# Rows of experts added up one pair behind their dots, ahead of each engine's step of the second half

## The chip, the cores and the metric

One core of a Trainium2 chip runs one program. TensorE (PE) multiplies, VectorE (DVE) does elementwise work, dot products and sorting, ScalarE (ACT) activation functions and scaled copies, GpSimd (POOL) issues the gathers, SyncE (SP) issues the weight loads. Each engine runs its own list of instructions in order and waits on semaphores for the others. The metric is the device time of the whole program in microseconds, the median of several executions.

## The reference

A block of layers over 512 tokens of width 1024: a short-convolution mixer and a feed-forward layer, a state-space mixer and a feed-forward layer, and then a hybrid layer of banded attention, a gated delta rule and a product-key layer of single-neuron experts. The change touches how the last two are interleaved. The product-key layer, cut to what matters (128 tokens in a block; 8 heads with 16 experts each):

```python
experts = jnp.take_along_axis(cand_i, pos, axis=-1)       # (128, 8, 16) of 16384
gates = jax.nn.softmax(top_s, axis=-1)
u  = expert_down[experts]                                 # a row of 1024 each
vv = expert_up[experts]
act = jax.nn.gelu(jnp.einsum("thkd,td->thk", u, hb))
out = jnp.einsum("thk,thkd->td", gates * act, vv)
```

So each of 4 blocks of 128 tokens has 128 experts per token. For each of them a row of 2048 numbers per token (`u` and `vv` side by side) is fetched, the first half is dotted with the token's vector, the result goes through GELU and the gate, and the second half is added to the output with that factor.

## The kernel before, in words

Everything is f32. After the first layers the hybrid layer is computed in two halves of 256 tokens. `pe_main(e, f)`, `act_main(e, f)` and `dve_main(e, f)` are generators: they give the work of half f on each engine in steps, and a step of one engine waits on semaphores for what the others made. Half 0 runs alone. Its tokens are blocks c = 0 and 1 of the experts; half 1 makes blocks 2 and 3. So while half 1 is still computed, the experts of block 0 and of part of block 1 are worked off between its steps.

`pe_experts`, `act_experts` and `dve_experts` write out that interleaving by hand. Block c has 64 rounds; a round `grp` handles a pair of experts per token (`GG = 2`), n = 128 c + 2 grp. In a round:

- POOL (`pool_gather`, a list of its own of 512 gathers) has fetched two tiles of 128 rows of 8 KB, 1 MB each, into a ring of buffers. Gather n waits until `g_mm` of the gather that had the buffer before it. Up to gather 255 there are `NRING = 7` buffers; from 256 on there are twelve, since five more have been freed by half 1.
- DVE: `dve_dots` (two CUSTOM instructions of 1024 elements, L187) waits for each gather and makes two columns of dots.
- ACT: `act_gelu` (128x2) waits for both dots. DVE: `dve_gate` (128x2 TENSOR_TENSOR, L170) multiplies by the gates. ACT: `act_diag` makes two 128x128 identities scaled by the factor of each token (L164, `arena<-arena,tail 128x128`).
- PE: `pe_add` (L153, `psum<-tail,arena ... 128x512`) multiplies each identity with the second half of its tile, two products of 512 columns each, and adds to two PSUM banks; f32 products count as two instructions in the profile, so the add of a pair is x8. Its end is `g_mm`, which frees the buffer.

Between them stands `steps_of(c, grp, main, ranks)`, a step of half 1 and steps of the ranking of the next block (`dve_topk`, 32 steps of top-16 searches on DVE; on PE and ACT it is nearly all waiting steps). In block 0 a round takes one step of half 1 (every fourth round two) and two of the ranking. In block 1 it takes half 1's steps first, and when they are at an end, the ranking for block 2; in block 2, the ranking for block 3. The ring of scaled identities has eight entries, that of dots eight pairs.

The order within a round is:

- PE: step, then `pe_add(grp)`.
- ACT: `act_gelu(grp)`, step, `act_diag(grp)`.
- DVE: `dve_dots(grp)`, step, `dve_gate(grp)`.

After the 64 rounds of a block, `pe_finish`, `act_finish` and `dve_finish` scale the sum, add the residual and free the PSUM banks; `store` is issued by ACT in round 4 of the next block (by SP for the last block). SP's list of weight loads (`sp_load`) knows nothing of rounds: it issues a load when the products that used the buffer are done.

Of the kernel before, what the change touches and what calls it, by code (L numbers as in the profile page):

```python
# [226 lines left out]
def build(nc, t, out):  # L227
    ctx = ExitStack()
    with ctx:
# [970 lines left out]
        def wait_steps(n):  # L1200
            for _ in range(n):
                yield
# [783 lines left out]
        def pe_tok(e, c):  # L1986
            for u in range(2):
                key = "htk", c, u
                o = ps.claim(key, QGB)
                e.wait_ge(*ps.vacant(key))  # L1990
                e.wait_ge(*t_h.at((5, c // 2, 7)))
                for k in range(4):
                    ins = e.tr(o[:, part[k]], H[:, 4 * u + k, part[c % 2]], ident)
                ins.then_inc(*tk_pe.tick((c, u)))
                yield
            yield

        def act_tok(e, c):
            yield
            for u in range(2):  # L2000
                e.wait_ge(*tk_pe.at((c, u)))
                if c > 1:
                    e.wait_ge(*g_dot.at(128 * (c - 2) + 127))
                e.act(htk[c % 2][:, 512 * u:512 * u + 512], ps["htk", c, u], ACT.Copy).then_inc(*ps.release(("htk", c, u)))
                yield
# [14 lines left out]
        def act_topk(e, c):  # L2020
            yield from wait_steps(31)
            e.wait_ge(*k_dve.at((c, "gate_in")))
            e.act(gates[c % 2], gates[c % 2], ACT.Exp).then_inc(*k_gate.tick(c))
            yield
# [125 lines left out]
        GROUPS = 128 // GG  # L2150
# [37 lines left out]
        def act_gelu(e, c, grp):  # L2188
            n = 128 * c + GG * grp
            d = dots[(n // GG) % 8]  # L2190
            e.wait_ge(*g_dot.at(n + GG - 1))
            e.act(d, d, ACT.Gelu).then_inc(*g_gelu.tick(n))

        def act_diag(e, c, grp):
            n = 128 * c + GG * grp
            d = dots[(n // GG) % 8]
            e.wait_ge(*g_act.at((c, grp)))
            for i in range(GG):
                if n + i >= 8:
                    e.wait_ge(*g_mm.at(n + i - 8))  # L2200
                e.act(diag[(n + i) % 8], ident, ACT.Copy, scale=d[:, i:i + 1]).then_inc(*g_diag.tick(n + i))

        def pe_add(e, c, grp):
            for i in range(GG):
                s_i = GG * grp + i
                n = 128 * c + s_i
                if s_i == 0:
                    for u in range(2):
                        ps.claim(("acc", c, u), (u,))
                        e.wait_ge(*ps.vacant(("acc", c, u)))  # L2210
                e.wait_ge(*g_in.at((c, s_i)))
                e.wait_ge(*g_diag.at(n))
                for u in range(2):
                    ins = e.mm(ps["acc", c, u], diag[n % 8], SLOTS[slot_no[n]][:, 1024 + 512 * u:1536 + 512 * u],
                               s_i == 0, s_i == 127)
                ins.then_inc(*g_mm.tick(n))

        def pe_finish(e, c):
            for u in range(2):
                o = ps.claim(("gB", c, u), HB)  # L2220
                e.wait_ge(*ps.vacant(("gB", c, u)))
                e.wait_ge(*der_ok.at((5, "post")))
                for k in range(4):
                    ins = e.mm(o[:, part[k]], post(5, 4 * u + k).broadcast_to([128, 128]), ident)
                ins.then_inc(*f_pe.tick(("gB", c, u)))
                o = ps.claim(("xo", c, u), HB)
                e.wait_ge(*ps.vacant(("xo", c, u)))
                for k in range(4):
                    ins = e.tr(o[:, part[k]], xT[:, 4 * u + k, 128 * c:128 * c + 128], ident)
                ins.then_inc(*f_pe.tick(("xo", c, u)))  # L2230

        def act_finish(e, c):
            for u in range(2):
                e.wait_ge(*f_pe.at(("gB", c, u)))
                if c:
                    e.wait_ge(*stored.at((c - 1, u)))
                e.act(fin_out[:, 512 * u:512 * u + 512], ps["gB", c, u], ACT.Copy).then_inc(*ps.release(("gB", c, u)))
# [13 lines left out]
        def store(e, c):  # L2251
            for u in range(2):
                e.wait_ge(*ps.done(("xo", c, u)))
                e.dma(out[0, 128 * c:128 * c + 128, 512 * u:512 * u + 512], fin_out[:, 512 * u:512 * u + 512]).then_inc(
                    *stored.tick((c, u), u))
# [10 lines left out]
        def steps_of(c, grp, main, ranks):  # L2266

            if c == 0:
                some(ranks, 2)
                some(main, 2 if grp % 4 == 3 else 1)  # L2270
            elif c == 1 and next(main, True) is None:
                pass
            else:
                some(ranks, 1)

        def pe_experts(e):
            main = pe_main(e, 1)
            before_rows(main, iter(()))
            for c in range(4):
                ranks = iter(()) if c == 3 else wait_steps(32)  # L2280
                late = pe_tok(e, 3) if c == 2 else iter(())
                for grp in range(GROUPS):
                    steps_of(c, grp, main, ranks)
                    next(late, None)
                    pe_add(e, c, grp)
                pe_finish(e, c)

        def act_experts(e):
            main = act_main(e, 1)
            before_rows(main, iter(()))  # L2290
            drive(act_topk(e, 0))
            for c in range(4):
                ranks = iter(()) if c == 3 else act_topk(e, c + 1)
                late = act_tok(e, 3) if c == 2 else iter(())
                for grp in range(GROUPS):
                    act_gelu(e, c, grp)
                    steps_of(c, grp, main, ranks)
                    next(late, None)
                    if c and grp == 4:
                        store(e, c - 1)  # L2300
                    act_diag(e, c, grp)
                act_finish(e, c)

        def dve_experts(e, ranks):
            main = dve_main(e, 1)
            before_rows(main, ranks)
            drive(ranks)
            for c in range(4):
                ranks = iter(()) if c == 3 else dve_topk(e, c + 1)
                late = wait_steps(3) if c == 2 else iter(())  # L2310
                for grp in range(GROUPS):
                    dve_dots(e, c, grp)
                    steps_of(c, grp, main, ranks)
                    next(late, None)
                    dve_gate(e, c, grp)
                dve_finish(e, c)

# [228 lines left out]
```

## Time and profile before

| | |
|---|---|
| median of 3 executions | 3680.81 us (3666.36 to 3682.61) |
| profiled execution | 3679.49 us, span 3677.7 us |
| mean granted clock of TensorE | 0.951 |
| busy | PE 3141.4 us (85%), DVE 2043.9 (56%), ACT 1178.7 (32%), POOL 562.0 (15%) |
| gathers | 512, 536.9 MB |

Times are in microseconds from the span's start. The engine names are followed by the line of the helper that issues the instruction, so L153 is every f32 product and the operands tell which. "idle before it <- X" is the time that the engine waited and the engine whose signal came last. A clock of 1.00 is TensorE's full rate of 2.4 GHz; the lower level is half of it, and a mean between them is a share of time at each.

### The profile page before, as it was taken

How to read it: one execution, taken by the hardware profiler on the slowest of the kernel's cores; microseconds unless marked ns; L12 is line 12 of the kernel's file. 1: busy time of each engine (PE TensorE's matmuls, PEld its weight loads, DVE VectorE, ACT ScalarE, POOL GpSimd, SP SyncE). 2: the span in 40 equal slices, each digit the busy share in tenths (PEclk: the TensorE clock that was granted, in tenths of full speed). 3: DMA queues.
4: the chain of work that ended last, by engine and by line, in shares of the span. 5: the costliest groups of instructions: out<-in, count | busy, mean ns of one | idle time of the engine just before them, and what ended most of it. 6: DMA issues, size and time to landing. Idle time of an engine off the chain costs nothing.

```text
span 3677.7 us, 34267 instructions
## 1 busy us (share of the span) xinstructions
PE 3141.4 (85%) x12402; PEld 2158.0 (59%) x12402; DVE 2043.9 (56%) x3974; ACT 1178.7 (32%) x2171; POOL 562.0 (15%) x540
## 2 busy tenths in 40 slices
PE   6989999798777989998988888977999777777777
PEld 4868888586555868886777635654565233223222
DVE  6654443776555454432552797554444878855554
ACT  3243222433444342223732345621222122211111
POOL 0000000000000000000000022212333444443332
PEclk9999999898888999998999989999999999999999
DMA  6534444242111424442303476867898999999998
GB/s 219 189 114 147 145 139 137 78 139 81 40 43 44 132 92 146 142 136 86 103 24 103 146 293 232 308 227 258 337 364 341 409 417 421 422 421 421 421 421 336
DMA packets 147543, 797.81 MB, mean 217 GB/s; under 512 B 16304, under 2 KB 18480, under 8 KB 81712
## 3 DMA queue, kind: packets, MB, share of 16 engines
q0 software_dynamic: 73728, 536.90, 36.8%
q1 hardware_dynamic: 69840, 251.69, 21.0%
q10 hardware_dynamic: 3808, 7.02, 0.5%
q8 instruction: 101, 1.65, 0.2%
q14 instruction: 66, 0.54, 0.0%
HBM read 793.46 MB, written 2.10 MB: 216 GB/s over the span
## 4 chain that ended last, share of the span: by engine, by line
PE 65%; DMA 17%; DVE 11%; ACT 4%; issue 3%; another core or an unknown queue 0%; POOL 0%; DVEq 0%; SPq 0%; ACTq 0%; POOLq 0%
PE psum L153 64%; DMA tail<-in_experts,tail 16%; DVE tail L187 2%; ACT arena L164 2%; DVE arena L182 2%; DVE tail L170 1%; ACT L164 1%; DVE tail L193 1%; PE psum L158 1%; DVE region L170 1%; DVE tail L190 1%; ACT region L164 1%; ACT tail L164 0%; DVE rounded L182 0%; DVE tail L196 0%
## 5 line engine op out<-in xcount | busy, mean ns | idle before, releaser
L153 PE MATMUL psum<-tail,arena 128*128 128x512 f32 (+2 forms) x3916 | 1386.7, 507 | 306.8 <-ACT arena L164 284.1
L153 PE MATMUL psum<-rounded,rounded 128*128 128x512 f32 x5496 | 1293.6, 396 | 40.1 <-DVE rounded L182 27.3
L153 PEld LDWEIGHTS psum<-tail,arena 128*128 128x128 f32 x3916 | 738.4, 196 | 916.8 <-issue 860.4
L153 PEld LDWEIGHTS psum<-rounded,rounded 128*128 128x128 f32 x5496 | 1036.6, 190 | 280.0 <-issue 56.2
L216 POOL DMA_INDIRECT tail<-in_experts,tail x512 | 541.9, 1058 | 1949.0 <-PE psum L153 977.9
L187 DVE CUSTOM_DVE_ANT_0 tail<-tail 128x1024 f32<-128x1024 f32 x512 | 621.4, 1225 | 351.7 <-DMA tail<-in_experts,tail 346.9
L170 DVE TENSOR_TENSOR rounded<-arena,rounded 128x1024 fp32r<-128x1024 f32 (+2 forms) x285 | 316.4, 1111 | 346.6 <-ACT rounded L164 346.4
L164 ACT ACTIVATE rounded<-arena 128x1024 fp32r<-128x1024 f32 (+2 forms) x317 | 291.9, 939 | 446.2 <-DVE arena L170 238.9
L164 ACT ACTIVATE tail<-tail 128x2 f32<-128x2 f32 (+1 forms) x288 | 64.1, 223 | 659.3 <-DVE tail L187 657.6
L164 ACT ACTIVATE arena<-arena,tail 128x128 f32<-128x128 f32 x512 | 177.6, 395 | 293.6 <-DVE tail L170 291.7
L164 ACT ACTIVATE arena<-psum 128x256 f32<-128x256 f32 (+2 forms) x210 | 97.8, 482 | 512.3 <-PE psum L153 512.0
L153 PE MATMUL psum<-arena 128*128 128x1 f32 (+3 forms) x792 | 197.6, 375 | 75.3 <-ACT arena L164 45.2
L164 ACT ACT_TABLE_LOAD x180 | 230.9, 1283 | 11.7 <-PE psum L153 6.4
L182 DVE SCALAR_TENSOR_TENSOR arena<-arena 128x512 f32<-128x512 f32 (+1 forms) x294 | 212.3, 724 | 21.7 <-ACT arena L164 10.9
L153 PEld LDWEIGHTS psum<-arena 128*128 128x128 f32 x792 | 127.5, 206 | 126.0 <-issue 82.1
L170 POOL TENSOR_TENSOR region<-region 128x256 f32<-128x256 f32 x24 | 19.9, 829 | 1130.6 <-DVE region L170 1130.6
L153 PE MATMUL psum<-tail 128*128 128x128 f32 (+4 forms) x888 | 138.9, 304 | 20.6 <-DVE tail L182 18.6
L153 PEld LDWEIGHTS psum<-tail 128*128 128x128 f32 (+2 forms) x888 | 108.8, 186 | 51.8 <-DVE tail L182 25.7
L170 DVE TENSOR_TENSOR arena<-psum,arena 128x512 f32<-128x512 f32 (+1 forms) x88 | 41.6, 476 | 168.2 <-PE psum L153 167.9
L182 DVE SCALAR_TENSOR_TENSOR arena<-psum,arena 128x511 f32<-128x511 f32 (+3 forms) x112 | 79.8, 713 | 97.2 <-PE psum L153 51.1
L170 DVE TENSOR_TENSOR tail<-tail 128x2 f32<-128x2 f32 (+5 forms) x299 | 95.7, 321 | 60.4 <-ACT tail L164 49.6
L164 ACT ACTIVATE arena<-arena 128x512 f32<-128x512 f32 (+3 forms) x138 | 80.6, 598 | 89.6 <-DVE arena L170 29.3
(82 smaller groups left out, 1452.5 us busy)
## 6 DMA issues: line engine op xcount, KB each, us to landing
arena<-in_ada SPq DMA_DIRECT2D x136, 512.0 KB
arena<-in_fin SPq DMA_DIRECT2D x88, 512.0 KB
arena<-in_win SPq DMA_DIRECT2D x56, 512.0 KB
arena<-in_fout SPq DMA_DIRECT2D x32, 512.0 KB
arena<-in_mxbc SPq DMA_DIRECT2D x32, 512.0 KB
arena<-in_pq SPq DMA_DIRECT2D x32, 512.0 KB
arena<-in_ain SPq DMA_DIRECT2D x24, 512.0 KB
arena<-in_mz SPq DMA_DIRECT2D x16, 512.0 KB
```

The costliest lines, as they stand in the source:

```text
L153: return self.e.matmul(o, a, b, start=start, stop=stop, skip_group_check=skip)
L158: return self.e.transpose(o, a, ident)
L164: return self.e.activation(o, a, func, bias=bias, scale=scale)
L170: return self.e.tensor_tensor(o, a, b, op)
L182: return self.e.scalar_tensor_tensor(out=o, in0=a, scalar=s, in1=b, op0=op0, op1=op1)
L187: return self.e.tensor_tensor_reduce(o, a, b, 1.0, 0.0, ALU.mult, ALU.add, total)
L190: return Unissued() if self.e is None else self.e.max(o, a)
L193: return Unissued() if self.e is None else self.e.max_index(o, m, a)
L216: return self.e.indirect_dma_start(out=o, out_offset=None, in_=table, in_offset=bass.IndirectOffsetOnAxis(ap=rows, axis=0))
```

## The change

The products and the factors of a pair move to the next round. With the rounds of all blocks counted through (`ALL_GROUPS`, 256 of them), round g is now:

- PE: step, then `pe_add(g-1)`.
- ACT: `act_gelu(g)`, `act_diag(g-1)`, step.
- DVE: `dve_dots(g)`, `dve_gate(g-1)`, step.

On ACT and DVE the gate and the identities thus also stand ahead of the step in place of behind it. The finish of a block moves with its last add into the first round of the next block, on DVE into the second round (`grp == 1`). After the last round the remaining add, and the finish of block 3, follow. The functions that are called are unchanged, and so are POOL's and SP's lists, the rings and all waits inside the functions.

```diff
--- before.py
+++ after.py
@@ -2273,47 +2273,61 @@
             else:
                 some(ranks, 1)
 
+        ALL_GROUPS = [(c, grp) for c in range(4) for grp in range(GROUPS)]
+
         def pe_experts(e):
             main = pe_main(e, 1)
             before_rows(main, iter(()))
-            for c in range(4):
-                ranks = iter(()) if c == 3 else wait_steps(32)
-                late = pe_tok(e, 3) if c == 2 else iter(())
-                for grp in range(GROUPS):
-                    steps_of(c, grp, main, ranks)
-                    next(late, None)
-                    pe_add(e, c, grp)
-                pe_finish(e, c)
+            for g, (c, grp) in enumerate(ALL_GROUPS):
+                if grp == 0:
+                    ranks = iter(()) if c == 3 else wait_steps(32)
+                    late = pe_tok(e, 3) if c == 2 else iter(())
+                steps_of(c, grp, main, ranks)
+                next(late, None)
+                if g:
+                    pe_add(e, *ALL_GROUPS[g - 1])
+                if g and grp == 0:
+                    pe_finish(e, c - 1)
+            pe_add(e, *ALL_GROUPS[-1])
+            pe_finish(e, 3)
 
         def act_experts(e):
             main = act_main(e, 1)
             before_rows(main, iter(()))
             drive(act_topk(e, 0))
-            for c in range(4):
-                ranks = iter(()) if c == 3 else act_topk(e, c + 1)
-                late = act_tok(e, 3) if c == 2 else iter(())
-                for grp in range(GROUPS):
-                    act_gelu(e, c, grp)
-                    steps_of(c, grp, main, ranks)
-                    next(late, None)
-                    if c and grp == 4:
-                        store(e, c - 1)
-                    act_diag(e, c, grp)
-                act_finish(e, c)
+            for g, (c, grp) in enumerate(ALL_GROUPS):
+                if grp == 0:
+                    ranks = iter(()) if c == 3 else act_topk(e, c + 1)
+                    late = act_tok(e, 3) if c == 2 else iter(())
+                act_gelu(e, c, grp)
+                if g:
+                    act_diag(e, *ALL_GROUPS[g - 1])
+                if g and grp == 0:
+                    act_finish(e, c - 1)
+                if c and grp == 4:
+                    store(e, c - 1)
+                steps_of(c, grp, main, ranks)
+                next(late, None)
+            act_diag(e, *ALL_GROUPS[-1])
+            act_finish(e, 3)
 
         def dve_experts(e, ranks):
             main = dve_main(e, 1)
             before_rows(main, ranks)
             drive(ranks)
-            for c in range(4):
-                ranks = iter(()) if c == 3 else dve_topk(e, c + 1)
-                late = wait_steps(3) if c == 2 else iter(())
-                for grp in range(GROUPS):
-                    dve_dots(e, c, grp)
-                    steps_of(c, grp, main, ranks)
-                    next(late, None)
-                    dve_gate(e, c, grp)
-                dve_finish(e, c)
+            for g, (c, grp) in enumerate(ALL_GROUPS):
+                if grp == 0:
+                    ranks = iter(()) if c == 3 else dve_topk(e, c + 1)
+                    late = wait_steps(3) if c == 2 else iter(())
+                dve_dots(e, c, grp)
+                if g:
+                    dve_gate(e, *ALL_GROUPS[g - 1])
+                if c and grp == 1:
+                    dve_finish(e, c - 1)
+                steps_of(c, grp, main, ranks)
+                next(late, None)
+            dve_gate(e, *ALL_GROUPS[-1])
+            dve_finish(e, 3)
 
 
 
```

## Rows read from the trace of the kernel before

**Rows 1.** The page: busy time of each engine, and the queue of the gathers.

```profile
...
PE 3141.4 (85%) x12402; PEld 2158.0 (59%) x12402; DVE 2043.9 (56%) x3974; ACT 1178.7 (32%) x2171; POOL 562.0 (15%) x540
...
q0 software_dynamic: 73728, 536.90, 36.8%
...
```

**Rows 2.** Busy time by engine in four stretches: granted clock, DMA share, GB/s last.

```profile
...
2106.00:2656.00 550.00, 466.06 (x1693) 280.29 (x1692) 343.83 (x831) 208.16 (x403) 140.14 (x131) 0.92 0.76 279
2656.00:2816.00 160.00, 151.97 (x573) 98.99 (x574) 66.96 (x132) 42.27 (x127) 50.24 (x44) 0.98 0.89 333
2816.00:3017.00 201.00, 150.39 (x318) 59.50 (x317) 158.75 (x406) 42.23 (x126) 89.44 (x80) 0.97 1.00 410
3017.00:3678.00 661.00, 491.65 (x1120) 199.44 (x1119) 401.80 (x868) 123.42 (x398) 257.66 (x253) 0.98 0.99 409
...
```

**Rows 3.** The chain that ended last, from 1950 us: start, us, what.

```profile
...
2128.04 7.98 DMA tail<-in_experts,tail
...
2852.44 9.12 DMA tail<-in_experts,tail
...
3108.45 22.96 DMA tail<-in_experts,tail
...
```

**Rows 4.** Waits from 2390 to 2550 us: who waited for whom, us, times, longest.

```profile
...
ACT arena L164 <- DVE tail L170: 96.2, 18, 10.4
...
DVE tail L170 <- PE psum L153: 59.8, 26, 5.8
PE psum L153 <- ACT arena L164: 33.8, 19, 2.9
...
```

**Rows 5.** Busy time by engine from 2390 to 2550 us, as in rows 2.

```profile
...
2390.00:2550.00 160.00, 125.58 (x575) 80.73 (x573) 86.38 (x160) 30.86 (x70) 31.83 (x34) 0.93 0.66 236
...
```

**Rows 6.** Timeline from 2470 us: start, duration, engine, instruction, idle before it.

```profile
...
2470.26 3.67 PE L153 MATMUL psum<-tail,arena 128*128 128x512 f32 x8 [1.38 <-ACT arena L164]
...
2473.78 3.73 PE L153 MATMUL psum<-tail 128*128 128x128 f32 x32
...
2477.55 1.28 DVE L170 TENSOR_TENSOR tail<-tail,psum 128x512 f32<-128x512 f32 x2 [0.50 <-PE psum L153]
2478.75 0.15 DVE L170 TENSOR_TENSOR tail<-tail 128x2 f32<-128x2 f32 x1
...
2478.94 0.69 ACT L164 ACTIVATE arena<-arena,tail 128x128 f32<-128x128 f32 x2 [6.73 <-DVE tail L170]
...
2479.49 3.67 PE L153 MATMUL psum<-tail,arena 128*128 128x512 f32 x8 [1.98 <-ACT arena L164]
...
```

**Rows 7.** Waits from 2245 to 2390 us.

```profile
...
PE psum L153 <- ACT arena L164: 4.7, 1, 4.7
```

**Rows 8.** Waits from 2550 to 2660 us.

```profile
...
PE psum L153 <- ACT arena L164: 10.5, 5, 6.5
...
```

**Rows 9.** Timeline from 2560 us: TensorE behind ACT's long chain.

```profile
...
2577.63 62.80 PE L153 MATMUL psum<-tail,arena 128*128 128x512 f32 x205 [6.48 <-ACT arena L164]
...
```

**Rows 10.** Waits from 2660 to 2815 us.

```profile
...
PE psum L153 <- ACT arena L164: 8.5, 4, 4.5
...
```

**Rows 11.** Timeline from 2943 us: dots, add, and the gathers issued behind it.

```profile
...
2943.80 1.23 DVE L187 CUSTOM_DVE_ANT_0 tail<-tail 128x1024 f32<-128x1024 f32 x1
...
2948.06 3.67 PE L153 MATMUL psum<-tail,arena 128*128 128x512 f32 x8 [1.28 <-ACT arena L164]
...
2948.77 1.23 DVE L187 CUSTOM_DVE_ANT_0 tail<-tail 128x1024 f32<-128x1024 f32 x1
...
2950.29 0.94 POOL L216 DMA_INDIRECT tail<-in_experts,tail  x1 [2.30 <-PE psum L153]
...
2952.01 0.94 POOL L216 DMA_INDIRECT tail<-in_experts,tail  x1 [0.78 <-PE psum L153]
...
```

**Rows 12.** Timeline from 2577 us: a gather's issue and the dot that waited for it.

```profile
...
2581.66 0.97 POOL L216 DMA_INDIRECT tail<-in_experts,tail  x1 [8.80 <-PE psum L153]
...
2587.49 1.23 DVE L187 CUSTOM_DVE_ANT_0 tail<-tail 128x1024 f32<-128x1024 f32 x1 [3.25 <-DMA tail<-in_experts,tail]
...
```

## The prediction

> **What bounds the kernel now.** I read the page first: TensorE is busy 85% of the span and no engine is full, so no single share decides [rows 1]. Then four stretches, cut at the dots of a pair, in which the 256 pairs of experts are worked off: 64, 24, 40 and 128 of them [rows 2]. The reader is to see two regimes. From 2106 to 2656 us (the 64 pairs of block 0, mixed with the second half's attention and delta rule) the DMA engines are busy 0.76 of the time; from 2816 on, with that work over, 1.00 and 0.99 at 410 GB/s. A gather is 1 MB (536.9 MB over 512, [rows 1]), and with the DMA full the second dots of pairs stand 4.97 us apart (2943.80, 2948.77) [rows 11]: 2.49 us a gather. The chain of what ended last agrees: a gather of 22.96 us followed by two products, again and again, near the end [rows 3]; a gather that takes 23 us stands in a queue of nine. So a microsecond saved before 2816 us brings everything after it forward by one, and behind 2816 us only a DMA engine that falls idle, or the last step, can change the time.
>
> Third, the waits of the stage in which the change can act, 2390 to 2550 us: PE waited 33.8 us, 19 times, for ACT's scaled identity, ACT waited 96.2 us for VectorE's gate, VectorE 59.8 us for PE [rows 4]: three engines in lockstep. TensorE was busy 125.6 of 160 us there, at a mean granted clock of 0.93 [rows 5]. The timeline shows one turn of it [rows 6]: PE adds a pair (2470.26, 3.67 us), does the second half's step (2473.78 to 2477.51), VectorE answers until 2478.83, only then multiplies by the gate (2478.75), ACT scales the identity (2478.94), and PE's next add starts at 2479.49, after 1.98 us idle.
>
> **The change, part by part.** It adds or removes no arithmetic, no transfer and no table load that the order forces; it moves three things in each of 256 rounds. VectorE's gate of pair g-1 and ACT's identities of g-1 come before the step, and PE's eight products of g-1 come after the step of round g. The loads of the second half are issued by SP from its own list, in the same order; the stores keep their place, on ACT in round 4 of a block. POOL's list of gathers is the same, but each waits for an add, and those come a round later.
>
> *Lockstep.* In the new order the add of g-1 needs identities that ACT can make as soon as VectorE has done the dots of g, while PE is in its own step. In the turn above: dots and gate take 2.5 us from 2478.8, identities and hand-over 0.8 more (gate to ACT 0.19, ACT to PE 0.55), so ready at 2482.1, while PE first adds the former pair (2477.5 to 2481.0) and then does the next step (3.73 us in this turn, to 2484.7) [rows 6]. VectorE's answer (1.3 us) hides behind the add. PE then has no gap. I take 31 of the 33.8 us, leaving a tenth for turns in which a gather comes late. Waits of the same kind are 4.7 us in 2245 to 2390 [rows 7] and 10.5 in 2550 to 2660 [rows 8]. Of the latter, 6.48 us are one wait behind ACT's long chain of logarithms and exponentials at 2577 [rows 9]; the identities of that pair would still stand behind that chain, so it stays. That gives 4 + 4 = 8 us.
>
> *Block boundary.* From 2660 to 2815 us PE waits 8.5 us for identities [rows 10], 4.5 of it where VectorE finishes block 0 before it starts on block 1; that finish now comes after the first dots. I take 4 us. The later boundaries lie under a full DMA queue and are worth nothing.
>
> *Clock.* The granted clock is 0.92 over 2106 to 2656, and 0.98 from 2656 to 2816, where PE is busy 95% [rows 2]. At two levels, 0.93 over 160 us means 22 us at the lower one, which cost 11 us. With the gaps gone part of it comes back: between 0 and 11, I take 5.
>
> *The ring.* This is the price. Until gather 255 there are seven buffers; a gather is issued when the add seven before it is done. Seven slots serve 3.5 pairs, so 3.5 P = L + hold, with P the time of a pair, L from issue to landing, hold from landing to the next issue into that slot. From the timeline at 2943 [rows 11]: the odd row of a pair lands at 2943.80 and its slot is refilled at 2952.01 (8.21 us); the even one landed 2.49 earlier and is refilled at 2950.29 (8.98); mean 8.6. Hence L = 17.4 - 8.6 = 8.8, and the chain shows 9.12 for such a gather [rows 3]; the sum closes. With the change the add starts 0.8 us after the second dot of the next pair (2948.77 + 1.23 + 0.8 = 2950.8 in place of 2948.06), so hold grows to 11.4, or 6.4 + P, and P = (6.4 + L)/2.5. What is the shortest L? 9.12 is mostly queue. A gather that found the queue short took 5.83 us (issued 2581.66, landed 2587.49) [rows 12], another 7.98, beside weight loads [rows 3]. The second of two issued 1.72 us apart waits 0.77 more, so the lower bound is a mean of 6.2 (P = 5.04), the upper 9.1 (P = 6.2). I take 6.9, nearer the lone one since in this stage there are no weight loads: P = 5.32 in place of 4.97, over the 40 pairs from 2816 to 3017 us: 14 us. The same over the eight pairs from 2656 to 2697: 3 us. In the first pairs of block 0, with their weight loads and slow adds: 4 us. Where PE is full the ring has room: the 16 pairs from 2697 to 2816 take 7.4 us each, and at P = 7.4 it allows L = 12.1. From gather 256 on there are twelve buffers: 29.8 - 11.4 = 18 us of room, so nothing.
>
> The Trainium skill speaks of the same quantity. "DMA: Bandwidth & Descriptors", section "Anatomy of one DMA", gives 2.0 us plus bytes by 436 GB/s, an estimate of 4.4 us here, by which the ring would cost nothing and the sum be 17 us lower; its section "Bandwidth" measures 6.15 us for 1 MB, by which the 40 pairs would cost 2 us. The trace's 5.83 and 7.98 us stand with the second.
>
> *The end.* Now the last gather is followed by dot, gate, identities and one add; with the change the add of pair 254 cannot start before that dot either, so one more back-to-back add lies on the path: 2470.26 to 2473.78, 3.5 us [rows 6].
>
> *Sum.* -31 - 8 - 4 - 5 = -48; +14 + 3 + 4 + 3.5 = +24.5; net -23.5 us. The profiled execution took 3679.5 us (span 3677.7), 1.3 below the median of the three runs, 3680.8. Forecast: **3656 us**.
>
> **Rivals.**
>
> *The ring bites harder.* If a gather cannot land in less than the 9.1 us of the chain, P = 6.2 and the 40 pairs cost 49 us, the eight 10, with 4 and 3.5 beside them: 66.5 against 48, so 3698 us, slower than before. It decides from L = 8.2 on (P = 5.84), where its costs equal the gains. For it: every gather of that stage showed about 9 us, and one with little before it showed 7.98. Against: 9 us is what seven buffers minus the held ones allow, and a gather was seen in 5.83.
>
> *The gaps only change their name.* If a step of PE needs VectorE's answer to the step before, and that answer is late because the dots in front of it now wait for a gather, PE idles before its step in place of before its add. Then the 39 us of gap savings and the 5 of clock are gone, and only 4 for the boundary stands against 24.5: 3700 us at worst; with half of the gaps and of the clock kept, 3678. For it: VectorE waited 59.8 us for PE in that stage, so the two are coupled. Against: VectorE was busy 86 of 160 us and has its answer ready 1.3 us after PE, against an add of 3.5.
>
> *The clock comes back in full and the ring is free.* Clock 11 in place of 5, L at the bound of 6.2 (3 us in place of 14, 1 in place of 3): 3679.5 - 54 + 11.5 = 3637 us.
>
> **How the numbers follow.** Forecast case 0.48 (its own range 3644 to 3668, from L of 6.5 to 7.5 and clock 0 to 11), clock and free ring 0.14, the gaps half or wholly renamed 0.22, the ring harder 0.16. A measurement of this kernel tells from no change about 0.5%, 18 us: faster means below 3662, slower above 3699. From the forecast case 0.38 of 0.48 lies below 3662, with all of the free-ring case 0.14 and 0.04 of the renamed one: 0.56. Slower: 0.06 of the ring case and 0.05 of the renamed one, 0.11. The rest, 0.33, is the same. The range reaches from just beyond the free-ring case, 3630, to just under the worst cases, 3696; that leaves about 0.06 below and 0.13 above.
>
> **What would show it.** Right: between 2390 and 2550 us PE's wait for ACT's identities falls below 5 us, PE is busy over 90%, and VectorE's last dots of block 0 come some 35 us earlier; in the 40 pairs without second-half work the DMA share falls to about 0.93 and a pair takes 5.2 to 5.4 us, with gathers of about 7 us in the chain where there were 9; from block 2 on a pair takes 4.97 us again; two adds, 7.2 us, stand behind the last dot. Wrong: gathers of 8 us or more in that stage, PE idle before its steps, or a DMA share there of still 1.00 (then the gain is larger).

## The result, and the profile after

| | before | after |
|---|---|---|
| median | 3678.78 us (3666.36 to 3682.61, 8 executions) | 3692.51 us (3683.08 to 3703.37, 8) |
| profiled execution | 3679.49 us, span 3677.7 | 3686.92 us, span 3685.1 |

The ratio is 1.0038, 95% interval 1.0025 to 1.0052: slower by 0.4%. That is less than the 0.5% that I had called measurable and inside the range of 3630 to 3696, but the interval excludes both no change and the gain that I forecast (3656). The change neither did nothing nor did only harm. It gained 34 us in block 0 and the start of block 1, and then gave back 40 us in the rest of block 1. The rows and tables of the two kernels are read from their profiled executions, which differ by 7.4 us where the medians differ by 13.7. In the runs further below two executions stand far outside and are left out of the ratios, one of the kernel before at 8078.24 us and one of best_again at 6345.27 us, without which the median of best_again is 3627.99.

The page of the kernel after, against [rows 1], shows the same engine shares. Its second line is VectorE's dots, with 525.9 us idle behind gathers; in the page of before that line has 346.9 us.

```profile
...
PE 3145.3 (85%) x12402; PEld 2157.1 (59%) x12402; DVE 2035.9 (55%) x3974; ACT 1152.8 (31%) x2171; POOL 592.4 (16%) x540
...
L187 DVE CUSTOM_DVE_ANT_0 tail<-tail 128x1024 f32<-128x1024 f32 x512 | 624.6, 1225 | 527.5 <-DMA tail<-in_experts,tail 525.9
...
```

The shares say next to nothing; the 179 us more behind gathers say where to look, not what they cost. The way to read it is by pairs. This table takes the start of the second dot of a pair (block, round) from both timelines:

| pair | before | after | after - before |
|---|---|---|---|
| (0,0) | 2110.16 | 2111.66 | +1.5 |
| (0,16) | 2248.60 | 2251.71 | +3.1 |
| (0,32) | 2393.55 | 2390.25 | -3.3 |
| (0,52) | 2567.95 | 2525.44 | -42.5 |
| (1,0) | 2657.84 | 2612.06 | -45.8 |
| (1,8) | 2698.91 | 2664.73 | -34.2 |
| (1,24) | 2819.19 | 2784.21 | -35.0 |
| (1,60) | 3004.63 | 3004.30 | -0.3 |
| (2,8) | 3066.16 | 3071.08 | +4.9 |
| (3,63) | 3664.39 | 3668.71 | +4.3 |

Busy time by engine in the kernel after, in four stretches cut at the pairs (0,0), (1,0), (1,24), (1,60); columns as in [rows 2], the granted clock, the DMA share and GB/s last. The last three rows are 2390 to 2510, which answers to [rows 5], then the whole stretch from (0,0) to (1,8), and the eight pairs from (1,0) to (1,8).

```profile
...
2106.00:2612.00 506.00, 440.21 (x1654) 267.86 (x1653) 344.92 (x829) 200.43 (x399) 143.17 (x127) 0.94 0.81 298
2612.00:2784.00 172.00, 160.81 (x616) 104.19 (x614) 66.96 (x134) 41.61 (x129) 54.06 (x49) 0.99 0.91 334
2784.00:3004.00 220.00, 157.91 (x285) 61.57 (x285) 151.10 (x391) 35.60 (x116) 80.21 (x71) 0.86 0.93 344
3004.00:3685.00 681.00, 504.74 (x1149) 203.41 (x1147) 400.44 (x882) 112.07 (x409) 290.27 (x261) 0.99 0.98 405
...
2390.00:2510.00 120.00, 113.97 (x582) 77.49 (x581) 82.70 (x154) 27.89 (x70) 41.02 (x35) 0.99 0.83 305
...
2112.00:2665.00 553.00, 479.89 (x1778) 289.04 (x1777) 369.17 (x878) 216.79 (x443) 158.02 (x141) 0.94 0.82 302
...
2612.00:2665.00 53.00, 45.68 (x154) 26.45 (x153) 26.46 (x54) 17.55 (x45) 17.11 (x17) 0.97 0.96 354
...
```

The same windows of the kernel before: (0,0) to (1,8), (1,0) to (1,8), (1,24) to (1,60).

```profile
...
2110.00:2699.00 589.00, 497.59 (x1770) 295.72 (x1771) 368.02 (x879) 223.58 (x445) 151.71 (x141) 0.92 0.77 284
...
2658.00:2699.00 41.00, 34.97 (x94) 18.19 (x95) 24.13 (x50) 16.68 (x43) 13.88 (x13) 0.92 0.88 353
...
2819.00:3005.00 186.00, 139.27 (x294) 55.09 (x292) 151.21 (x392) 39.40 (x116) 82.82 (x73) 0.96 1.00 410
...
```

Two things stand here. First, the lockstep (three engines waiting for one another in turn) is broken: from 2390 to 2510 TensorE is busy 114 of 120 us at a clock of 0.99, where [rows 5] had 126 of 160 at 0.93. Second, the stretch from (1,24) to (1,60), 36 pairs with no work of the second half, grew from 186 to 220 us, 5.15 to 6.11 us a pair, and the DMA engines moved 344 GB/s in place of 410.

The waits of TensorE from (0,0) to (1,8) in the kernel after, and then in 2370 to 2510 the two that answer to [rows 4]:

```profile
...
PE psum L153 <- ACT arena L164: 39.2, 17, 7.2
PE psum L153 <- DVE tail L182: 20.9, 9, 4.1
PE psum L158 <- DVE tail L182: 6.0, 2, 5.4
PE psum L153 <- DVE tail L170: 3.0, 3, 1.9
PE psum L158 <- issue: 2.4, 1, 2.4
...
DVE tail L170 <- PE psum L153: 18.9, 22, 4.0
...
PE psum L153 <- ACT arena L164: 4.8, 3, 2.4
...
```

The kernel before, waits of TensorE from (0,0) to (1,8):

```profile
...
PE psum L153 <- ACT arena L164: 72.6, 34, 7.4
PE psum L153 <- DVE tail L182: 18.6, 9, 3.9
PE psum L153 <- DVE tail L170: 0.6, 2, 0.4
```

The chain that ended last, kernel after, 2782 to 3004 us (start, us, what), first in full for a turn and then its gathers and adds:

```profile
...
2788.35 8.14 DMA tail<-in_experts,tail
2796.49 0.02 issue
2796.51 1.23 DVE tail L187 x2
2797.75 0.09 DVE tail L170
2797.83 0.06 issue
2797.89 0.40 ACT arena L164
2798.29 0.14 issue
2798.43 1.97 PE psum L153 x4
2800.40 0.26 issue
2800.66 7.25 DMA tail<-in_experts,tail
...
2868.84 6.40 DMA tail<-in_experts,tail
...
2877.17 2.69 PE psum L153 x4
...
2880.13 6.84 DMA tail<-in_experts,tail
...
2888.90 3.47 PE psum L153 x4
...
2934.27 8.85 DMA tail<-in_experts,tail
...
2945.05 1.97 PE psum L153 x4
...
2947.28 8.90 DMA tail<-in_experts,tail
...
```

This is the ring, closed into a loop. Pair g has the rows 2g (even) and 2g+1 (odd). The odd row lands, its dot is made, and only then do VectorE and ACT make the factors of pair g-1. Half of that pair's add (x4) frees the buffer of row 2g-2. With seven buffers, that buffer's next gather is seven rows on, 2g+5, the odd row of pair g+2. So one turn is two pairs: 2 P = L + 1.94 (landing to add) + 1.97 (half an add) + 0.26 = L + 4.17 us, at full clock. Of the 16 turns in this window 13 are of two pairs, 12.29 us on average (the other three span three pairs, 18.0 to 18.9 us); the 17 gathers of the chain take 6.40 to 8.90 us, 7.69 on average. Before, the add of pair g itself freed row 2g, so the loop spanned three pairs: with 6.49 us from the odd row's dot to the first gather behind its add ([rows 11], 2943.80 to 2950.29), L could be 3 x 4.97 - 6.49 = 8.4 us at the full rate of the DMA engines. After, it can only be 2 x 4.97 - 4.17 = 5.8, and no gather of the chain was that fast.

### The profile page after: what moved, and what is told of

It reads as the page before. It is cut to its first block, busy times and chain, and to the rows that moved or that the text cites. A ratio compares the mean times of both kernels' runs of the same rounds, so it can differ in the third digit from the quotient of the medians.

```text
span 3685.1 us, 34253 instructions
## 1 busy us (share of the span) xinstructions
PE 3145.3 (85%) x12402; PEld 2157.1 (59%) x12402; DVE 2035.9 (55%) x3974; ACT 1152.8 (31%) x2171; POOL 592.4 (16%) x540
## 4 chain that ended last, share of the span: by engine, by line
PE 64%; DMA 19%; DVE 10%; ACT 4%; issue 3%; POOL 0%; DVEq 0%; SPq 0%; ACTq 0%; POOLq 0%
PE psum L153 63%; DMA tail<-in_experts,tail 18%; DVE tail L187 3%; ACT arena L164 2%; DVE arena L182 2%; ACT L164 1%; DVE tail L170 1%; PE psum L158 1%; DVE region L170 1%; DVE tail L193 1%; ACT region L164 1%; DVE tail L190 0%; DVE rounded L182 0%; DVE region L182 0%; DVE arena L177 0%
## 5 line engine op out<-in xcount | busy, mean ns | idle before, releaser
L187 DVE CUSTOM_DVE_ANT_0 tail<-tail 128x1024 f32<-128x1024 f32 x512 | 624.6, 1225 | 527.5 <-DMA tail<-in_experts,tail 525.9
L216 POOL DMA_INDIRECT tail<-in_experts,tail x512 | 572.2, 1118 | 1928.7 <-PE psum L153 957.8
L164 ACT ACT_TABLE_LOAD x180 | 230.9, 1283 | 11.6 <-PE psum L153 6.3
L153 PE MATMUL psum<-tail 128*128 128x128 f32 (+4 forms) x888 | 136.9, 301 | 23.5 <-DVE tail L182 20.9
L153 PE MATMUL psum<-region 128*64 128x128 f32 (+2 forms) x560 | 78.8, 360 | 33.6 <-DVE region L170 32.6
```

Source lines behind the costliest of these rows:

```text
L153: return self.e.matmul(o, a, b, start=start, stop=stop, skip_group_check=skip)
L164: return self.e.activation(o, a, func, bias=bias, scale=scale)
L187: return self.e.tensor_tensor_reduce(o, a, b, 1.0, 0.0, ALU.mult, ALU.add, total)
L216: return self.e.indirect_dma_start(out=o, out_offset=None, in_=table, in_offset=bass.IndirectOffsetOnAxis(ap=rows, axis=0))
```

## Experiments

| label | what | median (executions) | ratio to before, 95% | us a pair, (1,24) to (1,60) |
|---|---|---|---|---|
| after | | 3692.51 (8) | 1.0038 [1.0025, 1.0052] | 6.11 |
| pe_only | TensorE's part alone | 3646.15 (4) | 0.9912 [0.9887, 0.9938] | 5.10 |
| factors_ahead | DVE's and ACT's part alone | 3809.68 (4) | 1.0359 [1.0332, 1.0387] | 6.11 |
| lag_block0 | change in block 0 only | 3646.74 (6) | 0.9919 [0.9896, 0.9942] | 5.22 |
| buf8_after | 8 buffers from gather 130 | 3652.80 (4) | 0.9930 [0.9904, 0.9957] | 5.08 |
| fill_after | added products in block 1 | 3688.68 (10) | 1.0026 [1.0011, 1.0040] | 6.03 |
| buf6_before | kernel before, 6 buffers | 3714.72 (5) | 1.0080 [1.0051, 1.0109] | 5.83 |
| buf6_after | after, 6 buffers | 3841.25 (4) | 1.0425 [1.0398, 1.0452] | 7.66 |
| buf11_before | kernel before, 11 from gather 130 | 3659.68 (7) | 0.9946 [0.9927, 0.9965] | 4.87 |
| buf11_after | after, 11 from gather 130 | 3637.74 (4) | 0.9895 [0.9867, 0.9924] | 4.99 |
| buf11_pe_only | pe_only, 11 from gather 130 | 3623.30 (4) | 0.9847 [0.9816, 0.9878] | 5.03 |
| best_again | the same, once more | 3631.54 (5) | 0.9867 [0.9838, 0.9897] | 5.01 |

The theory: the ring is one buffer short for the lag, and the lag that costs is that of the gate and the identities, which now stand behind the dots of the next pair. Its rival: the 40 us come from something else in the new order, TensorE's later add, its lower clock (0.86 there), or the loss of work that covered it.

### pe_only: TensorE's part alone

```diff
@@ dve_experts, against after
                 dve_dots(e, c, grp)
-                if g:
-                    dve_gate(e, *ALL_GROUPS[g - 1])
...
                 next(late, None)
+                dve_gate(e, c, grp)
@@ act_experts, against after
                 act_gelu(e, c, grp)
-                if g:
-                    act_diag(e, *ALL_GROUPS[g - 1])
...
+                act_diag(e, c, grp)
```

> Only TensorE's part of the change: its add of pair g-1 stands behind the step of round g, but VectorE's gate and ACT's identities of pair g stand behind the step of their own round, as before. Theory (ring): what keeps the buffers full in block 1 is that the gate of g-1 waits behind the dots of g, that is behind the next gathers. Here the identities of g-1 are ready before the next gathers land, and without a step in between the add starts at once; so block 1 runs at about 4.97 us a pair, the gaps of 2390 to 2550 us are closed all the same, and the time is 3640 us (3630 to 3650). Rival (delay): an add that stands one round later in TensorE's list frees its buffers later whatever feeds it; then block 1 costs 6.1 us a pair as in the changed kernel and the time is 3685 to 3695.

Measured 3646.15 us. Block 1 is at 5.10 us a pair, and the gain in block 0 is all there: (1,0) at 2610.8 us, 47 earlier than before. Its windows, eight pairs from (1,0) and then (1,24) to (1,60):

```profile
...
2612.00:2663.00 51.00, 46.95 (x157) 27.38 (x156) 26.19 (x54) 17.65 (x45) 18.53 (x18) 0.93 0.93 360
...
2780.00:2963.00 183.00, 137.50 (x290) 54.42 (x289) 150.44 (x391) 39.39 (x116) 82.80 (x73) 0.96 1.01 412
...
```

and its waits from 2370 to 2510 us, where a single wait of TensorE for ACT's identities is left, of 2.8 us (4.8 us in after):

```profile
...
ACT arena L164 <- DVE tail L170: 54.0, 18, 6.5
...
DVE tail L170 <- PE psum L153: 21.8, 24, 3.9
...
PE psum L153 <- ACT arena L164: 2.8, 1, 2.8
...
```

So TensorE's step of one pair ahead of its add is the whole gain, and moving gate and identities adds nothing to it. With work of the second half on TensorE the add comes after that step anyway; without it, in block 1, the add of g-1 starts as soon as its own identities exist, before the dots of g, and the ring is that of before.

### factors_ahead: VectorE's and ACT's part alone

```diff
@@ pe_experts, against after
-                steps_of(c, grp, main, ranks)
-                next(late, None)
                 if g:
                     pe_add(e, *ALL_GROUPS[g - 1])
...
+                steps_of(c, grp, main, ranks)
+                next(late, None)
```

> Only the other part: gate and identities of pair g-1 stand behind the dots of g and ahead of the step, and TensorE adds g-1 ahead of its step of round g, that is in the same place of its list as before the change. Theory (ring): the add waits for the dots of the next pair, so block 1 after the step of the second half takes 6.1 us a pair as in the changed kernel; and in 2390 to 2550 us TensorE's next step now waits for an add that waits for dots of the next pair, some 2 us more a round than before. Together 3740 us (3715 to 3765), slower than both. Rival (delay): TensorE's list is that of before, so block 1 is at 5 us a pair and the time 3680 to 3700.

Measured 3809.68 us, 70 us above what I expected: 6.11 us a pair in block 1, as expected and exactly that of after, and block 0 much worse, (1,0) 65 us later than before. About the stage of [rows 4] and [rows 5], the waits from 2400 to 2600 us and the window from 2397 to 2635:

```profile
...
DVE tail L170 <- PE psum L153: 104.7, 26, 9.4
PE psum L153 <- ACT arena L164: 67.2, 17, 5.2
...
2397.00:2635.00 238.00, 160.20 (x620) 96.35 (x620) 90.08 (x168) 31.18 (x79) 38.08 (x40) 0.85 0.49 178
...
```

Here TensorE waits for factors that wait for the dots of the next pair, and only then begins the step whose result VectorE needs: the lockstep at its strongest. So the half of VectorE and ACT alone makes the loss in block 1, wherever TensorE's add stands, and TensorE's half alone makes the gain in block 0.

### lag_block0: the new order for the first 64 pairs, the old one behind

```diff
+        LAG = 64
...
-                if g:
+                if g and g < LAG:
                     act_diag(e, *ALL_GROUPS[g - 1])
...
+                if g >= LAG:
+                    act_diag(e, c, grp)
```

The same on the other two engines.

> The new order in the 64 rounds of block 0 alone; then the pending pair is added, block 0 finished, and blocks 1 to 3 run in the order of before. Theory: the gain of 42 us up to the end of block 0 stays, the 4 us at the boundary go, and from block 1 on nothing is lost, since its gates no longer wait for the next gathers: 3640 us (3632 to 3650). Rival (the gain is borrowed: block 0 ends earlier with an emptier ring or with later half steps, and block 1 gives it back in any order): 3670 to 3680.

Measured 3646.74 us, block 1 at 5.22 us a pair. The loss is in block 1 and goes with the order there.

### buf8_after: one more buffer

Four more buffers of those that take over at gather 256 are free as soon as POOL has seen `mix_ok` (1, 1). One of them is put into the ring at gather 130.

```diff
-        slot_no = [n % NRING if n < 256 else (n - 256 + 256 % NRING) % len(SLOTS) for n in range(512)]
+        EXTRA, FROM, queue, slot_no = 1, 130, list(range(NRING - 0)), []
+        for n in range(512):
+            if n == FROM:
+                queue = [11 - i for i in range(EXTRA)] + queue
+            if n == 256:
+                queue[3:3] = [i for i in range(7, 12) if i not in queue]
+            slot_no.append(queue[0])
+            queue = queue[1:] + queue[:1]
...
+                if n == FROM:
+                    e.wait_ge(*mix_ok.at((1, 1)))
```

> The changed kernel with one buffer more, eight in place of seven, from the second gather pair of block 1 on (memory that the second half has by then left). Theory (ring): 4 P = 6.4 + P + L with L of 7.3 us gives P = 4.6, less than the 4.97 us that the DMA needs, so block 1 is bound by the DMA again or close to it (5.0 to 5.2), and the time is 3645 us (3636 to 3655). Rival (a slow clock of TensorE, or the order of VectorE's list, sets the 6.1 us): one buffer changes little, 3675 to 3690.

Measured 3652.80 us, 40 us less than after, from one megabyte. (1,24) to (1,60) of this kernel:

```profile
...
2792.00:2975.00 183.00, 135.92 (x290) 52.96 (x288) 150.09 (x392) 35.61 (x116) 84.95 (x73) 0.98 1.01 414
...
```

The DMA engines are full again and a pair takes 5.08 us. The eight pairs behind (1,0) still take 6.19 us each (6.58 in after), so one buffer does not cure them; why stands below.

### fill_after: the clock

Two products of 384 columns that nobody reads follow TensorE's add in each of the rounds 24 to 63 of block 1.

```diff
                     pe_add(e, *ALL_GROUPS[g - 1])
+                if 88 <= g < 128:
+                    o = ps.claim(("fill", g), (7,))
+                    e.wait_ge(*ps.vacant(("fill", g)))
+                    for u in range(2):
+                        ins = e.mm(o[:, 0:384], ident, xT[:, u, 0:384])
+                    ins.then_inc(*ps.release(("fill", g)))
```

> The changed kernel with two products of 384 columns more behind each add of rounds 24 to 63 of block 1, into a PSUM bank that nothing reads: work for TensorE in its idle time. In the changed kernel TensorE's mean granted clock there is 0.86 (0.97 before) and a pair takes 6.11 us. Theory (clock feeds back): the longer wait for gathers lets the clock fall, slower adds hold the buffers longer; with the fill the clock is above 0.95, a pair takes (6.4 + 7.3)/2.5 = 5.5 us, and the time falls by 20 to 25 us against the changed kernel, to 3669 (3662 to 3680). Rival (latency alone): the clock rises but a pair stays at 6.0 to 6.2 us and the time at 3690 or above, since the fill can only delay an add.

Measured 3688.68 us. The window of (1,24) to (1,60):

```profile
...
2790.00:3007.00 217.00, 179.13 (x434) 79.00 (x433) 150.98 (x392) 35.77 (x116) 86.71 (x74) 1.00 0.95 348
...
```

The clock went from 0.86 to 1.00, and a pair from 6.11 only to 6.03 us, as the rival said. From the dot of a row to the next gather into its buffer it took 0.8 us less (12.4 in place of 13.3), but from its issue to its dot a gather took 0.4 us longer (8.6 in place of 8.2). So the clock theory falls as the main cause: the higher clock gave back 3 of the 40 us. The added products can delay an add themselves, so that is what this fill brought and not all that a higher clock could.

### buf6_before and buf6_after: one buffer fewer

```diff
-        slot_no = [n % NRING if n < 256 else (n - 256 + 256 % NRING) % len(SLOTS) for n in range(512)]
+        EXTRA, FROM, queue, slot_no = 0, 130, list(range(NRING - 1)), []
...
```

> The kernel before the change with six buffers in place of seven in blocks 0 and 1 (eleven later). Theory (ring): 3 P = hold + L, hold 8.6 us in the pairs of block 1 with ranking, L not under 7.3 us, so P is 5.3 in place of 5.0 and block 1 costs some 12 us, the eight pairs before it 5: 3695 us (3688 to 3710). Block 0 with its 8.6 us a pair does not feel it. Rival (the number of buffers matters little, the order does): 3680.

> The changed kernel with six buffers in blocks 0 and 1. Theory (ring): 3 P = 6.4 + P + L, so P = (6.4 + 7.3)/2 = 6.9 us at full clock, 7.2 to 7.5 with the slower clock, in place of 6.1: 44 us in the 40 pairs, 8 in the eight before, and some 20 in the tight rounds of block 0, together 3765 us (3745 to 3790), so taking one buffer costs the changed kernel five times what it costs the kernel before. Rival (order does it, not the ring): 3692 to 3705.

Measured 3714.72 and 3841.25 us: with one fewer the old order loses 35 us and the new one 149. Both are more than the ring formula gave (3695 and 3765). More than half of the 149 us is lost before block 1: (1,0) stands at 2693.1 us, 81 later than in after, where I expected some 20. In block 1 of buf6_after, the chain that ended last and the window:

```profile
...
2920.68 7.91 DMA tail<-in_experts,tail
2928.61 1.23 DVE tail L187 x2
...
2930.52 6.17 PE psum L153 x8
...
2936.95 6.86 DMA tail<-in_experts,tail
...
2882.00:3158.00 276.00, 170.49 (x288) 68.40 (x288) 152.09 (x392) 35.73 (x116) 81.41 (x72) 0.77 0.73 275
...
```

With an even number of buffers it is the whole add (x8), not half of it, that frees the odd row's buffer, and at a clock of 0.77 it took 6.17 us in place of the 3.67 of [rows 6]. Odd gathers here took 7.97 us from issue to dot: 7.97 + 1.94 + 3.67 + 0.26 = 13.8, 6.9 us a pair at full clock. I put the rest up to 7.66 down to the slow adds; no run tests that here. The same loop for eight buffers spans three pairs: (7.7 + 5.9) / 3 = 4.5 us, below the 4.97 of the DMA engines, which fits the 5.08 of buf8_after.

### buf11_pe_only, buf11_after, buf11_before, best_again

All four free buffers enter at gather 130 (`EXTRA = 4`), under each of the three orders.

> TensorE's part of the change alone, and four buffers more from the second gather pair of block 1 on. With seven buffers the eight pairs at the start of block 1 took 6.4 us each and the rest 5.1. Theory (ring): with eleven the eight fall to 5.0 and the rest to 4.97, 11 + 5 us less than with seven: 3630 us (3624 to 3640). Rival (with seven the ring no longer binds, those pairs wait for the chain of the second norm): 3643 to 3648.

> The changed kernel with four buffers more, eleven in block 1 from its second pair of gathers on. With eight, a pair took 5.08 us in the 40 pairs and 6.2 in the eight before them, and the time was 3653 us. Theory (ring, cost entirely in block 1): 5.5 P = 6.4 + P + L gives room for L = 16, so 4.97 us a pair, and 5.0 to 5.5 in the eight: 3640 us (3632 to 3648), that is the gain of block 0 with only the last 3.5 us against it. Rival (part of the loss is the order itself): no better than with eight, 3650 to 3655.

> The kernel before the change with the same four buffers more in block 1. Its pairs there take 5.15 us on average against 4.97 at the DMA's rate, so there are 7 us to gain in the 40 pairs and 1 or 2 in the eight: 3671 us (3664 to 3679). Rival (the buffers are worth the 20 us that they brought to the kernel with TensorE's part of the change, whatever the order): 3659.

> TensorE's part alone with the eleven buffers once more, in five rounds: 3624 us (3618 to 3630), 0.985 of the kernel before.

Measured 3623.30, 3637.74, 3659.68 and, for the first once more, 3631.54 us. The best version of this study is TensorE's lag alone with eleven buffers, 1.3 to 1.5% faster than before. With eleven buffers the new order (3637.7) runs the 36 pairs at 4.99 us, so the 40 us are gone, and the order of pe_only is still ahead of it. The 16 pairs from (1,8) to (1,24), for which the prediction saw room in the ring, took 110.9 us there and 119.5 in after, so the ring held them a little too. Against the old order with the same buffers its block 1 is still slower: 335.9 against 327.7 us from (1,0) to (1,60). The old order gained 21 us from the buffers, not the 10 expected; the rival's 3659 is what came: its eight pairs from (1,0) took 4.46 us each in place of 5.13, (1,8) to (1,24) took 3.7 us less, and its block 1 has

```profile
...
2806.00:2982.00 176.00, 140.56 (x302) 56.62 (x301) 150.86 (x394) 39.54 (x117) 83.95 (x75) 0.97 1.01 422
...
```

422 GB/s, 4.87 us a pair. So seven buffers were a little short for the kernel before too. (In a stretch this short a pair can beat the 4.97 us of the prediction, since at (1,0) nine gathers were already under way or landed, where before it was five.)

## Why the prediction was partly right, and which step failed

Term by term, from the table of pairs (measured is the growth of the difference over the stretch):

| term | taken | measured |
|---|---|---|
| up to (0,0), not touched | 0 | +1.5 |
| first pairs of block 0, to (0,16) | +4 | +1.6 |
| waits up to (0,32) | -4 | -6.4 |
| lockstep and clock, to (0,52) | -31 - 5 | -39.2 |
| rest of block 0 and the boundary, to (1,0) | -4 - 4 | -3.3 |
| eight pairs to (1,8) | +3 | +11.6 |
| 16 pairs with TensorE full, to (1,24) | 0 | -0.8 |
| 40 pairs of the ring, to (2,8) | +14 | +39.9 |
| blocks 2 and 3 | 0 | -0.6 |
| the end | +3.5 | +3.1 |
| sum | -23.5 | +7.4 |

**What bounds the kernel, and where the change can act**: right. From (2,8) on nothing moved, and what was gained before arrived in full wherever the ring let it (pe_only).

**Lockstep**: right in place, mechanism and sum, but not in its parts. Up to (1,8), with the same work on TensorE (x1770 and x1778), the stretch shrank by 36 us. Waits for identities fell by 33.4 (72.6 to 39.2), but waits for VectorE's answers and for issue grew by 13.1, so TensorE idles only 18 us less (91.4 to 73.1); the other 18 are busy time (497.6 to 479.9) at a clock of 0.94 in place of 0.92. Busy time multiplied by the clock granted in it is 456 us before and 455 after: the work was the same and the clock is the whole of that part. The rival in which gaps only change their name came true for about two fifths of them, and the clock, which I had put at 5, made up for it. VectorE's wait for TensorE did not grow in the stage itself (18.9 against 59.8 in [rows 4]).

**The eight pairs**: taken as ring cost, 3 us, measured 11.6. In that stretch TensorE did 154 instructions in 45.7 us, where before it did 94 in 35.0 us: at (1,0) it was further behind VectorE's dots than before. The dots do not wait for TensorE (1.0 us), they wait for gathers. VectorE's wait from 2612 to 2665 us of after, and then from 2658 to 2699 of before:

```profile
...
DVE tail L187 <- DMA tail<-in_experts,tail: 28.2, 14, 3.8
...
DVE tail L187 <- DMA tail<-in_experts,tail: 14.2, 11, 2.2
...
```

The adds that free buffers stand behind TensorE's backlog, so gathers go out late: when the second dot of (1,0) starts, five gathers of later pairs have been issued in before, two in after and one in pe_only, which has the same backlog (46.9 of 51 us busy, x157) and takes 6.41 us a pair. lag_block0, where the pending pair is added at the boundary, has five again and takes 5.41. So it is the ring again, but short of gathers because TensorE is behind, and not for the reason that the prediction gave. The -45.8 at (1,0) thus overstates the gain, since it times VectorE while TensorE still has work left from before; -34.2 at (1,8) is what there was.

**The ring**: this is the step that failed, "I take 6.9, nearer the lone one", and with it P = 5.32 and 14 us. The mechanism, the place, the drop of the DMA share to 0.93 and even the rival's price (P = 6.2, 49 us) were right; the case that came was "the ring bites harder". The size was off in three parts, by the loop of the chain: the gathers took 7.69 us, not 6.9 (0.40 us a pair); the turn took 4.60 us beside them, not 4.17, because TensorE's clock was 0.86 and half an add took 2.45 us on average in place of 1.97 (0.22); and the loop that binds is that of the odd row, two pairs long, where I had averaged odd and even rows, which for L = 6.9 gives 5.32 in place of (6.9 + 4.17) / 2 = 5.54 (0.22). Together (7.69 + 4.60) / 2 = 6.15, against 6.11 measured. fill_after shows that the second part can't be had back by clock alone: when a buffer is refilled sooner, the gather finds more in front of it. Why L was not 6.9: gathers in this stage are issued in pairs 1.7 to 2 us apart ([rows 11], 2950.29 and 2952.01) with others of earlier pairs under way, and DMA engines busy 0.93 are not idle engines; the lone gather of [rows 12] went out after POOL had issued nothing for 8.80 us. The issues and landings in the trace of after bear that out. Of the 72 gathers of these 36 pairs, 8 were issued with one other still under way and took 6.3 us from issue to landing on average, 50 with two others and took 7.8, and 14 with three and took 8.9. In pe_only it is 7.5 us with two (8 gathers), 9.2 with three (58) and 10.5 with four (6). So the lone gather was the wrong row to lean on: none of these 72 was issued with nothing else under way. The median from issue to landing in 2784 to 3004 us is 7.9:

```profile
...
tail<-in_experts,tail POOLq DMA_INDIRECT x71, 7.9
```

The 6.15 us for 1 MB that the Trainium skill measures ("DMA: Bandwidth & Descriptors", section "Bandwidth") lies below all 17 gathers of the chain (6.40 to 8.90); it counts the time in which the DMA engines are busy and leaves out the making of the descriptors, which L has in it. The measurement decides. The formula of the Trainium skill's section "Anatomy of one DMA" gives 4.4 us, an estimate, and is further off.

**The end**: right. The kernel after, its last gather's dot and what follows (start, us):

```profile
...
3668.71 1.23 DVE L187 CUSTOM_DVE_ANT_0 tail<-tail 128x1024 f32<-128x1024 f32 x1 [1.13 <-DMA tail<-in_experts,tail]
...
3670.62 7.11 PE L153 MATMUL psum<-tail,arena 128*128 128x512 f32 x16 [1.27 <-ACT arena L164]
...
```

Two adds of 3.6 us stand back to back: 16.4 us from the last dot to the end of the span in place of 13.3. pe_only keeps the 13.3, since it makes the add of pair 254 in time.

**What stays open**: what, beside the number of gathers under way, sets the latency of a gather between 6.4 and 9 us here; why the lockstep cost factors_ahead and the six buffers cost block 0 so much more than expected; whether VectorE's gate or ACT's identities alone would do the harm, since both were always moved together; and how much of the loss in the eight pairs more buffers can take away (5.50 us a pair in buf11_pe_only against 6.41 in pe_only, but 4.46 in buf11_before). The start of block 1 differs by some microseconds from run to run of the same order: (1,0) stands at 2612.1 in after and 2618.3 in fill_after, whose added products come later.

## What to carry to other kernels

When work is moved one round back, ask of each engine's part apart whether it lengthens the time that a buffer is held, and close the ring as a loop in the chain of waits (this gather, this dot, half of that add, the gather into that buffer): how many rounds it spans and how long it takes decides, not a mean over slots. Take the latency in that loop from transfers as crowded as they will be, not from a lone one. Where the loop leaves less time than such a transfer takes (5.8 us against 7.7 here), try one buffer more before the reordering. And when a change has separable halves, try each alone: here one half alone gained 0.9% and the other alone cost 3.6%.

## What was not expected of the hardware

- A DMA share of 0.93 did not mean 93% of the rate: 344 GB/s, against 410 to 422 at a share of 1.00. Gathers of 8 KB rows kept the engines marked busy while they moved 16% less.
- Refilling a buffer sooner gave back less than it saved (fill_after): 0.8 us less from dot to refill, 0.4 us more from issue to dot.
- The more gathers were under way at its issue, the longer a gather took: in after 6.3 us behind one other, 7.8 behind two, 8.9 behind three.
- While TensorE did one add per pair and waited in between, the granted clock of the stretch was 0.86 in after (157.9 us busy of 220), 0.77 with six buffers (170.5 of 276) and 0.96 in the kernel before (139.3 of 186); with the added products it was 1.00 (179.1 of 217). An add of a pair took 3.67 us at full clock and up to 6.17 where it was lowest.
